# Two norms between a down projection and the next projection, worked by column halves

## The reference

```python
h = _layer_norm(DEEPNORM_ALPHA * h + _sq_relu_mlp(h, ffn_w1[layer], ffn_w2[layer]), ln_g[layer, 1], ln_b[layer, 1])
...
h = rmsnorm(x, norm_mix[layer])
proj = h @ w_in[layer]
```

## Time and profile before

| | |
|---|---|
| median of 3 runs | 2606.59 us (2606.41 to 2606.66) |
| the profiled execution | 2606.38 us |
| its span, first to last instruction | 2604.6 us |
| TensorE busy | 2583.1 us, 99% |
| VectorE busy | 1690.1 us, 65% |
| ScalarE busy | 1246.8 us, 48% |
| GpSimd busy | 191.6 us, 7% |

### The profile page before, as it was taken

The page is one execution under the profiler, slowest core; times in us unless marked ns, Lnnn a source line. Parts: engine busy times, 40 slices in busy tenths (PEclk is TensorE's granted clock), DMA queues, the critical chain, the costliest instruction groups (busy, mean ns, idle before and its releaser), DMA issues.

```text
span 2604.6 us, 42498 instructions
## 1 busy us (share of the span) xinstructions
PE 2583.1 (99%) x16507; PEld 2230.3 (86%) x16507; DVE 1690.1 (65%) x2938; ACT 1246.8 (48%) x2054; POOL 191.6 (7%) x240
## 2 busy tenths in 40 slices
PE   9999999999999999999999999999999999999998
PEld 9877799999999899879898776867877777899997
DVE  4544496265576566587265535886589987796786
ACT  4456365153265454465154334265354454475562
POOL 1111100000000000100000112061000000000000
PEclk9999999999999999999999999999999999999999
DMA  9995936957647665746557979922433333264452
GB/s 359 219 235 118 220 99 232 219 163 243 162 143 231 158 175 154 235 133 202 142 162 247 267 190 266 254 75 83 147 96 116 121 114 115 82 200 147 158 168 70
DMA packets 188778, 450.56 MB, mean 173 GB/s; under 512 B 15016, under 2 KB 33448, under 8 KB 187952
## 3 DMA queue, kind: packets, MB, share of 16 engines
q1 hardware_dynamic: 109424, 264.29, 30.0%
q0 software_dynamic: 60000, 167.78, 27.2%
q10 hardware_dynamic: 19168, 15.93, 2.1%
HBM read 438.24 MB, written 159.51 MB: 230 GB/s over the span
## 4 chain that ended last, share of the span: by engine, by line
PE 95%; DVE 3%; ACT 1%; issue 1%; DVEq 0%; ACTq 0%; POOL 0%; POOLq 0%
PE ps L399 32%; PE ps L1616 27%; PE ps L576 6%; PE ps L3550 4%; PE ps L3089 3%; PE ps L2531 3%; PE ps L2150 2%; PE ps L819 2%; PE ps L947 2%; PE ps L2315 2%; PE ps L2095 2%; PE ps L441 1%; PE ps L3772 1%; PE ps L2753 1%; PE ps L2074 1%
## 5 line engine op out<-in xcount | busy, mean ns | idle before, releaser
L370 DVE TENSOR_TENSOR w_lo<-raw,w_hi 128x1024 fp32r<-128x1024 f32 x500 | 611.3, 1224 | 459.7 <-ACT w_hi L362 458.6
L362 ACT ACTIVATE w_hi<-raw 128x1024 fp32r<-128x1024 f32 x500 | 527.1, 1055 | 499.0 <-PE ps L399 284.0
L1616 PE MATMUL ps<-x_hi,w_hi 128*128 128x264 f32 (+1 forms) x1120 | 317.2, 283 | 1.2 <-DVE rg L2029 0.7
L1616 PE MATMUL ps<-x_hi,w_lo 128*128 128x264 f32 (+1 forms) x1120 | 316.4, 282 | 0.0
L1616 PE MATMUL ps<-x_lo,w_hi 128*128 128x264 f32 (+1 forms) x1120 | 316.2, 282 | 0.0
L399 PE MATMUL ps<-x_hi,w_hi 128*128 128x512 f32 (+1 forms) x592 | 215.6, 380 | 0.7 <-ACT lq L2498 0.7
L1616 PEld LDWEIGHTS ps<-x_hi,w_hi 128*128 128x128 f32 x1120 | 210.8, 188 | 3.4 <-issue 2.2
L399 PE MATMUL ps<-x_lo,w_hi 128*128 128x512 f32 (+1 forms) x592 | 212.6, 375 | 0.0
L399 PE MATMUL ps<-x_hi,w_lo 128*128 128x512 f32 (+1 forms) x592 | 211.5, 373 | 0.0
L1616 PEld LDWEIGHTS ps<-x_hi,w_lo 128*128 128x128 f32 x1120 | 211.1, 188 | 0.0
L1616 PEld LDWEIGHTS ps<-x_lo,w_hi 128*128 128x128 f32 x1120 | 210.6, 188 | 0.4
(11 more groups left out here) (527 smaller groups left out, 6017.8 us busy)
## 6 DMA issues: line engine op xcount, KB each, us to landing
raw<-in_weights SPq DMA_DIRECT2D x255, 512.0 KB
raw<-weight_sums SPq DMA_DIRECT2D x280, 256.0 KB
weight_sums<-in_weights POOLq DMA_DIRECT2D x36, 1536.0 KB, 20.5
raw<-in_weights SPq DMA_DIRECT2D x210, 256.0 KB
weight_sums<-in_weights POOLq DMA_DIRECT2D x12, 2048.0 KB, 32.2
weight_sums<-in_weights POOLq DMA_DIRECT2D x12, 1792.0 KB, 22.8
weight_sums<-weight_sums POOLq DMA_DIRECT2D x12, 1536.0 KB, 14.3
weight_sums<-weight_sums POOLq DMA_DIRECT2D x4, 2048.0 KB, 20.0
```

What stands on the lines that cost most here:

```text
L362: nc.scalar.activation(w_hi[:, s], raw[:, s], ACT.Copy).then_inc(hi_ready, 1)
L370: nc.vector.tensor_tensor(w_lo[:, s], raw[:, s], w_hi[:, s], ALU.subtract).then_inc(lo_ready, 1)
L1616: last = nc.tensor.matmul(out_, w[:, s, 4 * (b % 2) + k], a, start=kind in "125" and k == n == 0, stop=k == 3 and n == 2, skip_group_check ...
```

## The change

The last two tiles of the down projection and the first four query tiles are each done in two halves of 256 token columns, and both norms are worked per half, in a new class `MixNorm` that takes the place of `ln11` and `rms_mix`.

- Down: chunks 12 to 15 are passed over twice, first for columns 0 to 255 of both tiles, then for the others. A chunk is signalled as done only in the second pass, which holds its slot of `w_hi` and `w_lo` until then.
- TensorE's sums are put between products: mean and variance of the first half inside the second pass of chunk 12, six of its eight squares after chunk 14, two inside chunk 15; those of the second half inside the first half's query products. VectorE now adds the last squares and tiles itself, so that mean and variance are one sum each. The squares of y have a place of their own (`y_squares`, the memory of `x_lo`). The fillers are gone.
- Queries: three tiles together (`FIRST` = 3), k by k, then the fourth, for the first half; the same for the second. The other four tiles as before.
- The mixing norm's scaled tile is (xc + b) times the root, and its gain is applied where `x_hi` and `x_lo` are made.
- y is written to x32 by GpSimd alone, after everything else of the norms; ScalarE waits for it ahead of the stage `latc`.

```diff
+        y_squares = nc.alloc_sbuf_tensor_at("y_squares", [P, KT, T], F32, offset=x_lo_start)
...
+        class MixNorm(LayerNorm):
+            NAME, NEXT, FIRST = "down1b", "latq", 3
...
+            def out(self, t, h):
+                b = 2 * ((self.down_tile + t) % 2) + h
+                return ps[:, b, 0:SEQ // 2]
...
+            def rms_pe(self, pe, h, pairs):
+                for k in range(2 * pairs[0], 2 * pairs[-1] + 2):
+                    pe.wait_ge(norm_squared, self.squares + KT * h + k + 1)
+                    last = nc.tensor.matmul(self.sum_out("rms", h), ones_d[:], self.square(k, h), start=k == 0, stop=k == KT - 1,
+                                            skip_group_check=True)
+                if k == KT - 1:
+                    last.then_inc(norm_var, 1)
+            def down_pe(self, pe, act_hi, act_lo, ready):
...
+                for h in range(2):
+                    for c in range(4):
...
+                            if h and (c, k) == (0, 3):
+                                self.mean_pe(pe, 0)
+                            elif h and (c, k) == (0, 7):
+                                self.var_pe(pe, 0)
+                            elif h and (c, k) == (2, 7):
+                                self.rms_pe(pe, 0, range(3))
+                            elif h and (c, k) == (3, 2):
+                                self.rms_pe(pe, 0, range(3, 4))
+            def latq_pe(self, pe):
...
+                for h in range(2):
+                    at = KT * (self.split + h)
+                    for t in range(self.FIRST):
+                        pe.wait_ge(lo_ready, self.latq + t + 1)
+                    pe.wait_ge(sum_added, self.sums_done(0) + 1)
+                    for k in range(KT + 1):
+                        if k:
+                            pe.wait_ge(norm_lo, at + k)
+                            for t in range(self.FIRST):
+                                last = products(t, k - 1, h, low)
...
+                        if k < KT:
+                            pe.wait_ge(norm_hi, at + k + 1)
+                            for t in range(self.FIRST):
+                                products(t, k, h, high)
+                        if h == 0 and k == 2:
+                            self.mean_pe(pe, 1)
+                        elif h == 0 and k == 4:
+                            self.var_pe(pe, 1)
+                    pe.wait_ge(lo_ready, self.latq + self.FIRST + 1)
+                    for k in range(KT):
+                        last = products(self.FIRST, k, h, high + low)
+                        if h == 0 and k == 3:
+                            self.rms_pe(pe, 1, range(3))
+                        elif h == 0 and k == 7:
+                            self.rms_pe(pe, 1, range(3, 4))
...
+            def down_act(self, act):
...
+                self.square_act(act, 6, 0)
+                self.square_act(act, 7, 0)
+                self.mean_act(act, 0)
+                split_hi(act, Step(self.latq))
+                self.root_act(act, 0)
+                split_hi(act, Step(self.latq + 1))
+                self.square_act(act, 6, 1)
+                self.rms_act(act, 0)
+                self.high_act(act, 0, range(4))
+                split_hi(act, Step(self.latq + 2))
+                self.square_act(act, 7, 1)
+                self.high_act(act, 0, range(4, 6))
+                self.mean_act(act, 1)
+                split_hi(act, Step(self.latq + 3))
+                self.high_act(act, 0, range(6, 8))
+                self.root_act(act, 1)
+                self.rms_act(act, 1)
+                self.high_act(act, 1, range(KT))
+            def centre_dve(self, dve, h):
...
+                    nc.vector.tensor_tensor(self.whole(k, h), self.whole(k, h), self.mean[:, c], ALU.subtract).then_inc(ln_centred, 1)
...
+            def down_dve(self, dve):
...
+                self.squares_sum(dve, range(4, 6))
+                self.add_dve(dve, 0, 0)
+                self.squared_dve(dve, 6, 0)
+                self.add_dve(dve, 1, 0)
+                self.squared_dve(dve, 7, 0)
+                self.centre_dve(dve, 0)
+                split_lo(dve, Step(self.latq))
+                self.scale_dve(dve, 0)
+                split_lo(dve, Step(self.latq + 1))
+                self.add_dve(dve, 0, 1)
+                self.squared_dve(dve, 6, 1)
+                self.rms_dve(dve, 0, range(4))
+                split_lo(dve, Step(self.latq + 2))
+                self.add_dve(dve, 1, 1)
+                self.rms_dve(dve, 0, range(4, 6))
+                self.squared_dve(dve, 7, 1)
+                self.centre_dve(dve, 1)
+                split_lo(dve, Step(self.latq + 3))
+                self.rms_dve(dve, 0, range(6, 8))
+                self.scale_dve(dve, 1)
+                self.rms_dve(dve, 1, range(KT))
+            def y_pool(self, pool):
+                pool.wait_ge(norm_scaled, KT * (self.n + 4))
+                c = slice(META, T)
+                for k in range(KT):
+                    nc.gpsimd.tensor_scalar(x32[:, k, c], self.xc[:, self.slot(k), c], par[:, self.b + k:self.b + k + 1], None, ALU.add).then_inc(norm_y, 1)
...
-            ln11.pool(pool)
-            pool.wait_ge(norm_lo, rms_mix.lo_at)
+            mix_norm.pool(pool)
+            pool.wait_ge(norm_lo, mix_norm.lo_at)
...
+            mix_norm.y_pool(pool)
...
-            keep_tiles(act, "latq", lq[:, :, META:T], scale=0.125)
+            mix_norm.latq_act(act, lq[:, :, META:T], 0.125)
+            act.wait_ge(norm_y, KT * (mix_norm.nl + 1))
...
-            mlp1.pe(pe, ln10, ln11)
-            ln11.pe(pe)
-            rms_mix.pe(pe)
+            mlp1.pe(pe, ln10, mix_norm)
```

More of the change, by code:

```diff
@@ L1473, in dve, with act @@
                         less_mean(later[k])
-                for k in range(self.Y_ON_ACT, KT) if self.last else ():
-                    dve.wait_ge(norm_scaled, KT * self.n + k + 1)
-                    nc.vector.tensor_scalar(x32[:, k, c], self.xc[:, self.slot(k), c], par[:, self.b + k:self.b + k + 1], None,
-                                            ALU.add).then_inc(norm_y, 1)
-            def act(self, act, follow=None):
+            def act(self, act):
                 c = slice(self.c0, T)
@@ L1764, in pe @@
                     self.first_banks_free(pe, f"seven{self.layer}{hn}")
-                    pe_stage(pe, f"down{self.layer}{hn}", self.h_hi, self.h_lo, self.wide,
-                             ready=(hidden_lo, 32 * self.layer + 16 * half), norm=next_norm if half else None)
+                    ready = (hidden_lo, 32 * self.layer + 16 * half)
+                    if half and self.layer:
+                        next_norm.down_pe(pe, self.h_hi, self.h_lo, ready)
+                    else:
+                        pe_stage(pe, f"down{self.layer}{hn}", self.h_hi, self.h_lo, self.wide, ready=ready, norm=next_norm if half else None)
             def act(self, act, next_norm):
@@ L1800, in act @@
                     self.seven_act(act, f"seven{self.layer}{hn}")
-                    if half:
+                    if half and self.layer:
+                        next_norm.down_act(act)
+                    elif half:
                         before_norm_act(act, f"down{self.layer}{hn}", next_norm)
@@ L1847, in dve @@
                     self.seven_dve(dve, f"seven{self.layer}{hn}", None if half else last_parts)
-                    if half:
+                    if half and self.layer:
+                        next_norm.down_dve(dve)
+                    elif half:
                         before_norm_dve(dve, f"down{self.layer}{hn}", 1.0, next_norm)
@@ L3890, in _ @@
             ln10.act(act)
[L3891 to L3893 removed]
+            mlp1.act(act, mix_norm)
             select_act(act)
```

203 lines of the change are left out of this document (181 added, 22 removed).

## The result

The changed kernel takes 2625.07 us (median of 4 runs, 2623.81 to 2627.8), the one before 2606.57 beside it: ratio 1.0072 [1.0055, 1.009]. That is slower by 18.5 us, where I had forecast 3.5, and outside my range.

What follows compares the result with a forecast made beforehand. TensorE, holding 95% of the chain, was taken as the bound: 54.0 of work plus 12.2 of waits and weight loads against 64.4 (+1.8), clock 1.7, queue nothing; 2606.4 + 3.5 = 2609.9, said 2610, range 2602 to 2616.

Steps and rivals of the forecast that it cites:

- New amount of TensorE work: Last down chunks to fifth query tile: 54.0 us of products and sums against 64.4, 10.4 to gain without waits.
- four waits: TensorE before the queries, at tile 6, after the second half's squares, before the fifth tile: 5.7, 2.7, 2.3, 1.1 us.
- the stretch: Last four down chunks to start of the fifth query tile: 66.2 us forecast against 64.4 before, +1.8.
- the first query product: TensorE starts it at t = 32.8, counted from 1461.02, having run dry at 27.0.
- The turn-taking: VectorE and GpSimd take turns when subtracting the mean from SBUF: 0.8 us of the 5.7 us wait before the queries.
- The clock: TensorE's clock falls to half after the wait before the queries: 1.7 us, bounds nothing and 2.3.
- the first wait: TensorE idle before the query products for 5.7 us, until three weight chunks are split.
- GpSimd's queue: y and the later weight-sum DMAs put the queue 15 us later; taken as nothing, up to 5 us at the upper end.
- The start: GpSimd's start of y, ahead of the weight sums' DMAs, moves from t = 50.4 to 59 to 62.
- the cover: Waits on GpSimd's queue that hide its delay: 18.7 us for line_rel, then 9.9 in front of the first combo.
- The rival on GpSimd's queue: Queue 15 to 21 us behind delays the first combo: 3 to 8 us on top of 3.5, 2613 to 2618; 27%.

Runs made afterwards that it cites:

- queue_early_fillers: queue_early plus 22, 6 and 7 throw-away TensorE products ahead of the three waits of the query tiles; 2610.17 us, ratio 1.0013.
- filler_first_wait: The changed kernel with 22 throw-away TensorE products ahead of the first wait only; 2624.07 us, ratio 1.0062.
- queue_early: The changed kernel with two weight-sum transfers on GpSimd's queue issued ahead of its wait for x_lo; 2614.39 us, ratio 1.0027.
- no_fillers: queue_early with query weight splits earlier, second half's additions behind scaling, mean read from PSUM, sums of squares moved, no throw-away products; 2604.10 us.
- before_queue_half_late: The kernel before the change with four 128x512 additions put in GpSimd's queue; 2608.32 us, ratio 1.0003.
- y_on_vector: The changed kernel with the eight y additions made by VectorE, not GpSimd; median 2620.98 us, profiled execution 2613.79.
- before_queue_late: The kernel before the change with eight 128x512 additions put in GpSimd's queue; 2615.54 us, ratio 1.0034.

## Why the prediction was wrong

- **New amount of TensorE work, four waits**: right in kind and place, each wait ended by what I had named. 5.7, 2.7, 2.3 and 1.1 us were forecast, 6.5, 2.2, 2.2 and 0.6 measured, 11.4 in all against 11.8. With the clock held the stretch is 67.3 to 67.9 (queue_early_fillers, filler_first_wait), where I had 66.2: 1.1 to 1.7 too low. The miss lies before the first query product, which I had at t = 32.8 and which came at 34.45: TensorE ran dry 0.9 us later than I had it, 0.4 of that in a wait for the squares that I had left out, and waited 0.8 longer. The turn-taking, which I took as 0.8 us, cost VectorE 2.5, because GpSimd's subtractions met VectorE's last three and the split behind them; how much of it reaches the wait is not shown. Three of my differences don't follow from the times beside them, either: 32.8 - 27.0 is 5.8, 53.6 - 51.5 is 2.1 and 66.0 - 65.1 is 0.9, 11.5 in all, which changes nothing here.
- **The clock, taken as 1.7, bounds 0 to 2.3**: it fell, as I had chosen, but the bound was too tight. The short course of one fall cost about 1.0 (queue_early 68.3, queue_early_fillers 67.3), the long one with a second fall about 4. I had allowed only for the first wait. And the granted clock shows the falls here, though it read 1.00 at the start of the program. The Trainium skill (TensorE: Matmul & The Clock Gate, Part 1) says that idle time takes the clock to half. The traces agree for the first wait: the four profiles in which it is 6.5 to 6.7 us long all have 0.50 behind it. Behind the waits of 2.2 us the clock fell in two of them and not in the other two, nor in filler_first_wait and no_fillers.
- **GpSimd's queue, the step that failed.** Three sizes in it were too small. y: "between 0.35 each and 1.26", taken as 6 us in all, was 14.87; my upper end was a price of another form, and 1.86 lies above it. The start: t = 59 to 62 forecast, 65.3 measured (1528.06). So the weight sums' first issue came 31.5 us later than before, not 15. Then the cover. I wrote that only the 9.9 us and TensorE's own delay cover it if the line's transfer stands behind the copies, and yet put 0 into the sum. The chain's last link starts 28.5 us late (1712.23 against 1683.71); less TensorE's own 8.6 and less 9.9 that is 10.0, and VectorE's wait grew by 10.64 - 0.68 = 9.96. The other 2.8 of the 12.8 can only in part be TensorE's half clock after that wait (0.57 from 1710 to 1720): with the clock at 1.00 and the first combo only just late, before_queue_half_late and y_on_vector lose 1.1 and 1.7 us on top of what VectorE's wait grew by. The rival on GpSimd's queue was the right one in mechanism, but its 3 to 8 us belonged to a queue 15 to 21 us behind.
- **The chances**: by its own condition, over 12 to 14 us behind, the rival was already met by the 15 us of my own estimate. It should have been the forecast.

## What to carry to other kernels

A wait in front of a DMA issue is slack only if nothing that was issued before it is still in the way: compare the time from issue to landing with the wait, and follow the chain of transfers to the first compute instruction that someone waits for. Price work put on a queue against that end, not against the first idle time behind it. And where a late queue sets the end, improvements upstream show in the time only as far as they let the queue start earlier; mend the queue first, and measure them then.

## What the runs showed of the hardware

- An addition with a per-partition scalar on GpSimd, 128x512 fp32, takes 1.86 us (8 in 14.87), about 2.0 in before_queue_late (8 in 15.79). GpSimd's subtraction of two tiles of that size takes 1.25 in the kernel before (3 in 3.75), less, though it reads more.
- The clock at 145 to 155 us fell to 0.83 in some executions and not in others, with the same work there; the rebuilt stretch then starts 1.1 to 1.9 us later.
- After a wait of 2.2 us the granted clock fell only sometimes: not in no_fillers and filler_first_wait, but in the changed kernel (0.66 in 1510 to 1515), 7 us after it had risen from a first fall.
- The transfer of the 40 KB line was issued behind four weight-sum transfers. The DMAs that wait for it came 38.9 to 42.6 us after the issue of these, whether the line was issued 3.7 or 23.3 us into that time.
- VectorE and GpSimd hold each other up where both read two SBUF tiles (1.31 us instead of 0.75 for two subtractions), and not where VectorE takes one operand from PSUM.
- Fillers longer than the wait cost what they overrun: 40 in place of 22 made the stretch 2.5 us longer together with the other two groups (69.8 and 67.3).
